# One layer of a hybrid encoder block: an expert's load and a chunk's load change places in the SyncE queue, and two score matmul groups change their order

## The reference

```python
h = rms_norm(x, gain)
dq, dk, dv, gq, gk, gv, beta, dec, gate, ma, mb = split(h @ w_in)    # 1024 x 5640
y_a = diff_attention(dq, dk, dv)        # 4 heads, two score maps of 64 dims each
y_b = gated_delta_net(conv(gq), conv(gk), conv(gv), beta, dec, gate)  # 4 heads, chunks of 64
x = x + (sigmoid(ma) * (y_a @ w_a) + sigmoid(mb) * (y_b @ w_b)) @ w_out
x = x + hier_moe(rms_norm(x))           # 32 experts, 2 chosen for each token
y = rms_norm(x) * final_gain
```

## Time and profile before

| | us |
|---|---|
| median of 3 runs | 490.68 (488.63 to 491.43) |
| the profiled execution's own time | 491.43 |
| its span | 489.7 |
| PE busy | 449.2 |
| PE weight loads busy | 339.3 |
| DVE busy | 206.0 |
| ACT busy | 123.7 |
| loaded | 137.13 MB, mean 280 GB/s |

### The profile page before, as it was taken

One profiled execution on the slowest core, in us unless ns is written; L12 is line 12 of the kernel. 1 busy time (PEld: TensorE's weight loads), 2 busy tenths in 40 slices (PEclk: granted clock), 3 DMA queues, 4 the chain that ended last, 5 costly groups with the idle time before them and its releaser, 6 DMA issues.

```text
span 489.7 us, 10288 instructions
## 1 busy us (share of the span) xinstructions
PE 449.2 (92%) x4337; PEld 339.3 (69%) x4337; DVE 206.0 (42%) x588; ACT 123.7 (25%) x311; POOL 12.9 (3%) x37
## 2 busy tenths in 40 slices
PE   9999999999999899999999799999988787797794
PEld 8885698875888799888545576767665654556551
DVE  1367287996344460702201554344352143412324
ACT  5002423001031321220013633323232122212234
POOL 6011000000000000000000000000000000000000
PEclk9999999999999999999999999999999788987899
DMA  8969936416413131344598579999999999999972
GB/s 312 387 198 360 406 115 206 146 43 200 171 30 143 26 147 21 153 173 171 209 423 328 241 308 421 416 422 417 422 416 421 418 424 418 419 421 418 420 322 91
DMA packets 37601, 137.13 MB, mean 280 GB/s; under 512 B 8496, under 2 KB 9840, under 8 KB 25392
## 3 DMA queue, kind: packets, MB, share of 16 engines
q1 hardware_dynamic: 33056, 134.70, 69.5%
q10 hardware_dynamic: 4352, 1.21, 1.1%
q0 software_dynamic: 144, 0.52, 0.3%
HBM read 134.59 MB, written 1.84 MB: 279 GB/s over the span
## 4 chain that ended last, share of the span: by engine, by line
PE 63%; DMA 21%; DVE 10%; SPq 2%; issue 2%; ACT 1%; ACTq 0%; DVEq 0%
PE ps L843 22%; DMA arena<-in_moe_w_up 12%; PE ps L1160 8%; DMA ring<-in_moe_w_up 6%; PE ps L1067 6%; PE ps L1052 6%; PE ps L1129 3%; PE ps L1215 3%; PE ps L1205 3%; PE ps L861 2%; DVE arena L1530 2%; DVE arena L1527 2%; DMA arena<-in_w_in 2%; PE ps L1169 2%; SPq L363 1%
## 5 line engine op out<-in xcount | busy, mean ns | idle before, releaser
L843 PE MATMUL ps<-arena 128*128 128x256 f32 (+1 forms) x640 | 157.7, 404 | 0.7 <-DMA arena<-in_w_in 0.7
L843 PEld LDWEIGHTS ps<-arena 128*128 128x128 f32 x640 | 120.5, 191 | 30.8 <-issue 15.7
L1160 PE MATMUL ps<-arena 128*32 128x128 f32 x1088 | 42.4, 300 | 14.0 <-DMA arena<-in_moe_w_up 13.0
L1160 PEld LDWEIGHTS ps<-arena 128*32 128x32 f32 x1088 | 32.6, 117 | 22.9 <-DMA arena<-in_moe_w_up 16.1
L1160 PE MATMUL ps<-ring,arena 128*32 128x128 f32 x960 | 36.8, 296 | 9.8 <-DMA ring<-in_moe_w_up 7.6
L1160 PEld LDWEIGHTS ps<-ring,arena 128*32 128x32 f32 x960 | 28.7, 116 | 17.1 <-DMA ring<-in_moe_w_up 9.0
L656 ACT ACTIVATE arena<-ps 32x256 f32<-32x256 f32 x62 | 23.4, 377 | 56.1 <-PE ps L1205 55.7
L1129 PEld LDWEIGHTS ps<-arena 128*128 128x128 f32 x256 | 30.7, 200 | 3.4 <-issue 3.4
L1129 PE MATMUL ps<-arena 128*128 128x128 f32 x256 | 32.2, 286 | 0.8 <-DVE arena L1748 0.8
L1826 DVE COPY arena<-ps 32x256 f32<-32x256 f32 x62 | 25.8, 417 | 11.6 <-PE ps L1205 10.2
L1067 PE MATMUL ps<-arena 128*128 128x512 f32 x64 | 28.3, 595 | 0.0
(11 more groups left out here) (266 smaller groups left out, 457.2 us busy)
## 6 DMA issues: line engine op xcount, KB each, us to landing
arena<-in_w_in SPq DMA_DIRECT2D x9, 2048.0 KB, 9.1
arena<-in_moe_w_gate SPq DMA_DIRECT2D x17, 1024.0 KB, 25.5
arena<-in_moe_w_up SPq DMA_DIRECT2D x17, 1024.0 KB, 26.6
arena<-in_moe_w_down SPq DMA_DIRECT2D x16, 1024.0 KB, 23.5
ring<-in_moe_w_gate SPq DMA_DIRECT2D x15, 1024.0 KB, 24.7
ring<-in_moe_w_up SPq DMA_DIRECT2D x15, 1024.0 KB, 26.0
ring<-in_moe_w_down SPq DMA_DIRECT2D x15, 1024.0 KB, 26.2
arena<-in_w_out SPq DMA_DIRECT2D x2, 2048.0 KB, 7.9
```

Source lines behind the costliest of these rows:

```text
L843: last = pe.matmul(out, lhs, rhs, start=(k == 0 and (i > 0 or part % 2 == 0)), stop=(k == KD - 1), skip_group_check=(i == 0))
L1160: last = pe.matmul(c.ps[ROWS * q:ROWS * (q + 1), i % 2, 0:P], c.Hg[par][:, k, ROWS * i:ROWS * (i + 1)], c.gu_w[slot][:, :, k, start:start ...
```

## The change

Two edits. On SyncE, `load_expert(0)` is moved from behind chunk 1 to the loop that loads experts 1 and 2, and chunk 2 from its place between the two blocks of small rows to the place right behind expert 0. All thirteen small loads now stand between chunk 1 and expert 0, and none of them stands behind the wait for gk. On TensorE, `scores` goes through map 0 for all four heads and then through map 1, in place of taking the two maps in turn for each head; each map's entry is waited for right before its own matmuls.

```diff
     load_chunk(0)
     load_chunk(1)
-    load_expert(0)
 ...
     row(c.gdng, io["gdn_norm_gain"][0:1, :], "vectors_loaded")
-    load_chunk(2)
     for i, nm in enumerate(("q1", "k1", "q2", "k2")):
 ...
     sp.dma_start(c.gffn, io["norm_ffn_gain"][0].rearrange("(p k) -> p k", k=KD)).then_inc(s["router_loaded"], 16)
-    for j in range(1, OWN):
+
+    for j in range(OWN):
         load_expert(j)
         load_chunk(2 + j)
     load_chunk(5)
 ...
         pe.wait_ge(s["dk_ready"], 1)
-
-        outs = [side(f"s{qt}{m}").rearrange("p (h k) -> p h k", h=H) for m in range(2)]
-        for h in range(H):
-            for m, ps in enumerate(outs):
-                rows = slice(DH * m, DH * (m + 1))
+        for m in range(2):
+            ps = side(f"s{qt}{m}").rearrange("p (h k) -> p h k", h=H)
+            rows = slice(DH * m, DH * (m + 1))
+            for h in range(H):
                 last = pe.matmul(ps[:, h, 0:P * (qt + 1)], c.qT[rows, h, qt * P:(qt + 1) * P],
                                  c.kT[rows, h, 0:P * (qt + 1)], start=True, stop=True)
-                if h == H - 1:
-                    last.then_inc(s["side_ready"], 1)
+            last.then_inc(s["side_ready"], 1)
```

## The result

The changed kernel takes 493.41 us, the median of 14 runs (491.79 to 497.02), beside 491.37 us for the kernel before (14 runs, 488.63 to 494.04). The ratio of the two is 1.0054, 95% interval 1.0034 to 1.0076: slower by some 2.65 us (1.7 to 3.7); the two medians themselves lie 2.04 us apart. The forecast had said 0.9 us slower, too little to measure; the time lies inside its range, but the loss is two to three times the size forecast, near what rival 2 had priced (3.1 us).

The account below looks back on a forecast made before the run. Bound by a serial chain of TensorE to gv, VectorE's inverse, ma0's chunk and TensorE, then weights at 419 GB/s. Median 490.68 + 1.0 (chunk 2 late) - 0.1 (edit two) = 491.6 us; range 489.3 to 494.0.

Parts of the forecast that it names:

- rival 2: Small loads: the row block runs one load at a time, chunk 2 3.2 us late; 493.8, or 495.5 with clock fall; chance 0.14.
- What bounds it: Whole kernel: TensorE to gv, VectorE's inverse, ma0's chunk and TensorE in series; a microsecond before 240 us reaches the end.
- Chunk 2's deadline and its direction: Front: TensorE wants chunk 2 at 37.06 us; behind expert 0 and small loads it lands later, at 38.1 us.
- Chunk 3: Front: waits for gq as before, lands no later than before, and costs nothing.
- Chunk 2 late by +1.0 us: TensorE's first matmul on chunk 2: a wait of 1.0 us, bounds 0 to 3.2 us.
- The laid-over sequence: SyncE's queue: the old small-load pattern laid over the start; expert 0 issued at 21.6 us, chunk 2 landing 16.5 later.
- Rival 4: TensorE's clock: the half-clock stretch at 47 us does not fall where it did; -1.7 us, 489.9; chance 0.09.
- Edit two: Score groups: 2.2 us more on TensorE, hidden by waits; sum -0.1 us, +2.2 if uncovered, -0.3 at best.
- The covers: TensorE behind scores(0) and scores(1): waits of 0.69 and 1.63 us hide the longer score groups.
- earlier release: Score groups: map 0 done first lets VectorE start 0.14 us earlier for each; nothing won at scores(0), -0.14 at scores(1).
- Rival 3: Score groups: weight loads laid bare add 1.0 us in each, both late by 1.0 and 0.8; 493.4 us; chance 0.05.
- Rival 1: Front: small loads pass under chunk 1 and chunk 2 comes in time; 490.6 us; chance 0.22.

Follow-up runs that it names:

- e6: Changed kernel with experts 0 and 1 (6.3 MB) ahead of chunk 2; ratio 1.0236 to the kernel before.
- e1: Changed load order with the old order of the score matmuls; ratio 1.0062 to the kernel before.
- e11: The changed kernel run once more, unchanged, for another profile; ratio 1.0066 to the kernel before.
- e7: Changed kernel with only the two loads of the router's weights (2,048 pieces) moved behind chunk 2; ratio 1.0064 to the kernel before.
- e4: Changed kernel with the router's five loads behind chunk 2, eight rows and expert 0 ahead; ratio 0.9995 to the kernel before.
- e5: Changed kernel with expert 0's third load (down) behind chunk 2, 2.1 MB of it ahead; ratio 0.9998 to the kernel before.
- e12: Changed kernel with eight of ten row loads reading 128 different rows of w_in, other values computed; ratio 0.9992 to the kernel before.
- e3: Changed kernel with chunk 2 issued ahead of expert 0, all small loads still ahead of both; ratio 0.9995 to the kernel before.
- e10: Kernel before with ma0's chunk issued when the inverses are stored, not when loaded back; ratio 1.0006 to the kernel before.
- e9: Kernel before with the new score order and map 1's four matmuls done three times over; ratio 1.0089 to the kernel before.

## Why the prediction was right in its mechanism and wrong in its size

**What bounds it: held.** A delay ahead of gv reaches the end whole (e6: 9.33 us of wait and 2.45 of clock become 11.8 at the expert part, and 11.7 in the time). The weight stream keeps its 420 GB/s. One link of the chain is not the usual one: TensorE waits for ma0's chunk (0.68 us) in the profile of before and in none of the others. In the pair of profiles shown above, TensorE is 4.65 us later at gv (68.40 us against 63.75) and 3.71 at the expert part, and this wait, absent after, is most of the difference.

**Chunk 2's deadline and its direction: held.** It was wanted at 37.1 us, came late, and TensorE's wait at its first matmul is where the time went. Chunk 3, said to land no later, landed 1.0 us later (37.20 + 16.8 = 54.0 us against 52.99), and nothing waited for it.

**Its size: this is the step that failed.** "Chunk 2 late by +1.0 us" measured 2.3 to 3.0 us by its landing (39.3, 39.5 and 40.1 us against 37.06), with waits of 1.8 to 3.0 us. The laid-over sequence was sound from expert 0's issue on: 16.5 us forecast from there to the landing, 15.8 (e1, e11) to 16.4 measured. What was off is that issue itself, 21.6 us forecast and 23.5 to 23.8 measured. The prediction took the nine-load block of before for the thirteen-load block of after and let two corrections cancel: four more rows (+2.2 us, its own upper bound) against 7 us more for SyncE to queue them under chunk 1. The second doesn't exist. SyncE did queue all rows by 14 us, yet from the sixth on they pass about one a microsecond after chunk 1 has ended, so having been queued early buys them nothing. The 533 packets in one microsecond, on which the hope of quick rows rested, were nearly all packets of the four rows that are quick in the changed order too. Had the 2.2 us been added, the term would have been 3.2 us, the upper end and rival 2's value. That this fits is in part luck. The four rows themselves took 1.1 us, not 2.2 (their landings, 16.90 to 18.01 us), and from there to expert 0's issue the other nine loads took 5.7 us (5.9 in e1, 5.3 in e11), not the 4.8 us taken over from before.

**The clock: weighed in rival 2, and seen behind two of four waits.** Behind the 2.97 us wait of the changed kernel the clock fell (1.64 us lost there), and behind e7's 3.01 us (0.53 from 40 to 42 us, 1.55 us lost); behind 1.78 (e11) and 2.39 us (e1) it did not. Over 40 to 70 us the mean clock is 0.94 in before, e1 to e4 and e7 to e11, wherever the lower stretch lies; it is 1.00 in e5 and e12, which have none there. So in e7 the fall behind the wait came in place of the usual stretch and cost nothing net. Only the changed kernel (0.89) and e6 had two stretches of that kind, and the second one's 1.6 us is a good part of why the changed kernel's profiled execution lost 4.9 us and the ratio says 2.65. Rival 4, that the stretch doesn't fall at 47 us, came true in e3 and e4 (60 to 64 us) and was worth nothing, since it moved and did not go. Nor is bdg's delay what moves it: in e3 and e4 nothing waits for chunk 2, and in e10, with the load order of before, the stretch lies at 60 to 64 us too.

**Edit two: right.** Its cost on TensorE was overstated (2.2 forecast, 0.54 + 0.98 = 1.5 measured), perhaps since the two halves still overlap where one map gives way to the other, which no run shows by itself. The covers held it, with some 0.3 us left of the first and 0.8 of the second (e9). The 0.14 us of earlier release did not show: VectorE starts on map 0 2.12 us after scores(1) starts, before it was 2.11 us, though eight passes at 0.216 us are done by 1.73; why, no run here tells. (VectorE starts 0.11 us behind the group's end in the rows of before, 165.32 against 163.21 + 2.00, not 0.05.) Rival 3, weight loads laid bare on one row group, is refuted by e9: 16 more passes on one half run at 0.216 us each, the full-height pace, loads hidden. The Trainium skill ("TensorE: Matmul & The Clock Gate", Part 3, The mechanism) says in one sentence that a weight load overlaps only when the row groups differ, which would have made them slower; the same section also has a load for the background weight buffer pulled ahead, which would not. The measurement decides: they were not slower.

**Rival 1 (small loads pass under chunk 1)** fell with the 18 to 22 us stretch. **Left open:** the timed loss of the load order is 2.65 to 3.2 us in three comparisons (changed, e1, e11). In e1 and e11, whose profiles have one lower stretch as before, TensorE starts on chunk 2 only 2.5 and 2.3 us later; in the changed kernel it is 3.1 us and a second stretch. The intervals (1.7 to 4.6 us) don't tell whether something else adds a few tenths.

## What to carry to other kernels

A bulk prefetch whose data isn't needed for a long time belongs behind every load with a deadline, not ahead of it, and the margin is to be counted in bytes: here 3.1 MB ahead of chunk 2 were affordable behind eight rows, with 0.9 us to spare (e4), and no longer behind all thirteen small loads. Count small loads that copy one row to all partitions as about a microsecond of queue time each, and add them load by load rather than let them cancel against slack that wasn't shown. Work that grows in front of a wait is free up to that wait's length, and the profile names that length, here 0.2 to 0.3 us short.

## What the runs showed that was not expected

- Six loads that read one row 128 times took 0.9 to 1.0 us each of an otherwise idle queue (87 to 121 packets in a microsecond), while the router's 2,048 pieces of 16 and 128 bytes passed at up to 1,827 in one. With eight of the ten rows read from 128 places of another tensor, all ten landed within 2.1 us and not 6.7.
- SyncE's issue of a load ran far ahead of the queue: rows were issued by 14 us and landed until 23.6, and what held SyncE (6.70 us) was the load behind them.
- Matmuls of 64 rows on one half of the array run at 0.112 and 0.216 us a pass at 128 and 256 columns, with the two halves in turn at 0.069 and 0.12.
- TensorE's granted clock fell to the lower level (1.2 GHz) behind the waits of 2.97 and 3.01 us and within that of 9.33, and not behind those of 1.63, 1.78 and 2.39 us. The matmuls behind the wait then took 1.6 to 2.5 us longer; in one of the three (e7) this came in place of the stretch that most profiles have later, in the other two on top of it.
